# Modulation rows summed in PSUM under the down stages, and eight more up tiles as seven block products

## The chip, the cores and the metric

One core of one Trainium2 chip runs the whole program in one launch. The metric is the device time of an execution in microseconds; the kernel before has a median of 2543.47 us over three runs (2543.4 to 2543.87).

## What is computed

A sequence of 512 tokens of width 1024 passes two layers and a second block. Each layer has a gated FFN (width 2816), a mixer (attention in layer 0, a spatial gating unit in layer 1) and a second gated FFN; each of the three is preceded by an RMS norm that is scaled and shifted by rows of a modulation vector, and followed by a gate from the same vector. All arithmetic is float32.

```
c_act = silu(c)
for i in range(2):
    mod = c_act @ ada_w[i] + ada_b[i]            # 9 rows of 1024: shift, scale, gate, three times
    sh1, sc1, g1, sh2, sc2, g2, sh3, sc3, g3 = split(mod, 9)
    h = rms_norm(x, ln_ffn1[i]) * (1 + sc1) + sh1
    x = x + 0.5 * g1 * ((silu(h @ wg) * (h @ wu)) @ wd)
    ...                                          # mixer with sh2, sc2, g2; second FFN with sh3, sc3, g3
    x = rms_norm(x, ln_out[i])
```

The second block (a gated recurrence, an MLP with squared relu, a last norm) is not touched by the change, nor are the mixers.

## The kernel before

**Tiles.** A float32 product is made of three TensorE products of rounded parts: `hi*hi`, `hi*lo`, `lo*hi`. A weight tile is 1024 x 256, 1 MB. SyncE (SP) loads it to one of two slots of `w_raw`, ACT casts it to `w_hi_t` (`conv`, `cast_piece`, L1110, L1123), GpSimd (POOL) subtracts to get `w_lo_t` (L931, L937). The token operand is held as `h_hi` and `h_lo`, the FFN's hidden layer as `act_hi` and `act_lo`. A standard tile (`unit`, L2320 to L2325; at some places `unit_part`, L2337 to L2342) is two units of 24 products with 512 columns.

**Seven block products.** The other form of an up tile (`seven_tile`, L2377 to L2380) cuts weights and tokens into 2 x 2 blocks and makes seven products of blocks instead of eight, in the manner of Strassen: 84 TensorE products with 256 columns. In return other engines add blocks. On the weights: pieces 3, 4 and 6 of a tile (counted from 0) are sums made by DVE (`piece_sum`, L1818 to L1822) in PSUM banks 6 and 7, cast by ACT (`cast_piece`) and split by DVE (`piece_low`, L1828). On the tokens: four turned operands `t_hi_t` and `t_lo_t` are made once per FFN (`t_op`), in the down stage before the first such tile (`turns`) or, in a group of both forms, beside its standard tiles. On the results: ACT copies block results out of PSUM to `hidden` as they come (`snap`, L1131 to L1137), DVE adds them (`row_sum`). Product 3 of a tile waits for the copy of its product 0, product 6 for the fourth copy. `seven_act` writes out ACT's order: the copies of a tile alternate with the casts of the next tile's pieces; for the first tile of a stage, pieces 4 to 6 are cast at the end of the down stage, before the first copy.

**FFN stages.** An FFN goes through its 2816 hidden columns in three groups of 8, 8 and 6 up tiles (gate and up weights in turn), each followed by a down stage of four tiles that adds to `x`. Each unit of a down stage ends in one bank; DVE adds it to `x` (L2025), eight updates per stage, and TensorE may use the bank again two units later. In the loop over these updates `down` on DVE also has what is hung onto single updates: modulation steps, the turning, and, after updates 5 and 7 (counted from 0) where seven-product tiles follow, the first tile's pieces. `std` in the plan says how many tiles of a group are standard: all 22 in layer 0's first FFN, 8 (the first group) in layer 0's second and layer 1's first, 4 in layer 1's second.

**Modulation.** Sixteen rows of 1024 (`ada_block`) remain after the start. Each is summed by DVE in eight steps: SP loads 128 x 1024 of `ada_w` (512 KB) to one of four slots of `ada_raw`, DVE multiplies it with a column of `c_act` and adds it to an accumulator in `scr` (`ada_step`, L1678 and L1681). After the eighth step DVE transposes blocks (L1688) and reduces (L1689); TensorE adds over partitions (`ada_sums`, L2501), and DVE adds the bias and derives gains (`ada_fin`). The steps lie in the up stages of layer 0's first FFN (24, 24, 16), its first two down stages (12, 12), the first up stage of layer 0's second FFN (24) and of layer 1's first (16). The accumulators and slots lie in the part of `scr` that the turned operands use later, so these groups have standard tiles.

**Order.** Every engine runs one list in order, written out by the loops over `ops`; semaphores tie the lists. SP's list has the weight loads and the steps' loads in one queue. In layer 1's first FFN DVE also scales `x` by the last norm (`scale_x`, L1809), three blocks after each pair of up tiles.

## Time and profile before

| | |
|---|---|
| median of 3 runs | 2543.47 us |
| the profiled execution | 2543.58 us |
| its span, first to last instruction | 2541.7 us |
| TensorE busy | 2500.6 us, 98% |
| DVE, ACT, POOL busy | 58%, 44%, 44% |
| granted TensorE clock, mean | 0.994 |
| DMA | 312.52 MB, 123 GB/s over the span |
| modulation loads | 128 of 512 KB, 6.1 us to landing |

Times in the profile are microseconds from the span's start unless marked ns. PE is TensorE, POOL is GpSimd, SP is SyncE. In a timeline a line is: start, duration, engine, line, operation, output<-inputs, shapes, count, and in brackets the idle time of the engine before it and who ended it. Matmuls are pipelined, so start-to-start spacing is what one costs, not its duration.

### The profile page before, as it was taken

To read this page: it belongs to the slowest core of one execution; us is meant where nothing else is said; L and a number is where in the kernel's file an instruction comes from. 1 tells how busy PE (TensorE), PEld (TensorE's weight loads), DVE (VectorE), ACT (ScalarE), POOL (GpSimd) and SP (SyncE) were. 2 spreads that over 40 slices of the span, in tenths; PEclk is the share of its full clock that TensorE was granted. 3 is DMA by queue.
4 is the path that set the end of the run, shared out by engine and by line. 5 is a ranking of instruction groups with operands and counts; after the bars stand their busy time and mean duration, and the time that the engine had idled before them with its cause. 6 is when DMAs were issued, how large, how long until landed. Compare 5 with 4: busy or idle time off the path is not lost.

```text
span 2541.7 us, 36310 instructions
## 1 busy us (share of the span) xinstructions
PE 2500.6 (98%) x14578; PEld 2182.6 (86%) x14578; DVE 1466.4 (58%) x2045; ACT 1109.9 (44%) x1933; POOL 1112.6 (44%) x578
## 2 busy tenths in 40 slices
PE   6999999999999999999999999999999999999999
PEld 5888888776888989889998988999988888889998
DVE  6767674445577635767455258453566555564543
ACT  3222224565523635425445335454554444434544
POOL 2455444232446655456564435565640000455553
PEclk8999999999999999999999999999999999999999
DMA  8687754221372333543323322333232221223322
GB/s 297 223 274 244 244 195 129 67 67 50 116 243 90 115 100 96 180 139 100 114 86 100 118 83 67 117 100 133 92 101 86 67 67 50 92 92 114 103 84 83
DMA packets 249244, 312.52 MB, mean 123 GB/s; under 512 B 7356, under 2 KB 227149, under 8 KB 248950
## 3 DMA queue, kind: packets, MB, share of 16 engines
q1 hardware_dynamic: 246762, 308.88, 36.9%
q8 instruction: 116, 1.90, 0.3%
q10 hardware_dynamic: 2316, 1.33, 0.2%
q14 instruction: 50, 0.41, 0.1%
HBM read 308.07 MB, written 4.74 MB: 123 GB/s over the span
## 4 chain that ended last, share of the span: by engine, by line
PE 92%; DVE 4%; DMA 1%; issue 1%; ACT 1%; POOL 0%; SPq 0%; DVEq 0%; ACTq 0%
PE bank L2320 12%; PE bank L2325 12%; PE bank L2321 12%; PE bank L2377 8%; PE bank L2380 8%; PE bank L2378 8%; PE bank L2337 6%; PE bank L2338 5%; PE bank L2342 5%; PE bank L2303 2%; PE bank L2305 1%; PE bank L2304 1%; PE bank L2392 1%; PE bank L2393 1%; PE bank L2394 1%
## 5 line engine op out<-in xcount | busy, mean ns | idle before, releaser
L937 POOL TENSOR_TENSOR w_lo_t<-w_raw,w_hi_t 128x1024 fp32r<-128x1024 f32 (+1 forms) x284 | 713.9, 2531 | 1163.4 <-ACT w_hi_t L1110 1162.9
L1110 ACT CAST w_hi_t<-w_raw 128x1024 fp32r<-128x1024 f32 (+1 forms) x316 | 311.1, 1026 | 368.5 <-PE bank L2325 175.7
L931 POOL TENSOR_TENSOR w_lo_t<-w_raw,w_hi_t 128x512 fp32r<-128x512 f32 x232 | 323.3, 1409 | 240.3 <-ACT w_hi_t L1123 238.1
L2320 PE MATMUL bank<-act_hi,w_hi_t 128*128 128x512 f32 x720 | 280.9, 390 | 1.5 <-DVE x L2025 1.3
L2320 PE MATMUL bank<-h_hi,w_hi_t 128*128 128x512 f32 x720 | 281.3, 391 | 0.6 <-ACT hidden L1377 0.6
L2321 PE MATMUL bank<-act_lo,w_hi_t 128*128 128x512 f32 x720 | 280.2, 389 | 0.0
L2321 PE MATMUL bank<-h_lo,w_hi_t 128*128 128x512 f32 x720 | 280.2, 389 | 0.0
L1681 DVE SCALAR_TENSOR_TENSOR scr<-scr,cact 128x1024 f32<-128x1024 f32 x112 | 215.0, 1920 | 62.8 <-DMA scr<-in_ada_w 54.8
L2377 PE MATMUL bank<-t_hi_t,w_hi_t 128*128 128x256 f32 x928 | 232.8, 283 | 0.0
L2378 PE MATMUL bank<-t_lo_t,w_hi_t 128*128 128x256 f32 x928 | 232.7, 283 | 0.0
L2025 DVE SCALAR_TENSOR_TENSOR x<-bank,half,x 128x512 f32<-128x512 f32 x88 | 65.9, 749 | 222.8 <-PE bank L2325 152.5
L1123 ACT CAST w_hi_t<-bank 128x512 fp32r<-128x512 f32 x174 | 102.3, 588 | 189.8 <-PE bank L2325 63.4
L2325 PE MATMUL bank<-act_hi,w_lo_t 128*128 128x512 f32 x720 | 178.7, 389 | 0.1
L2377 PEld LDWEIGHTS bank<-t_hi_t,w_hi_t 128*128 128x128 f32 x928 | 178.2, 192 | 0.0
L2378 PEld LDWEIGHTS bank<-t_lo_t,w_hi_t 128*128 128x128 f32 x928 | 178.2, 192 | 0.0
L2325 PE MATMUL bank<-h_hi,w_lo_t 128*128 128x512 f32 x720 | 177.8, 389 | 0.0
L2377 PE MATMUL bank<-h_hi,w_hi_t 128*128 128x256 f32 x696 | 174.5, 283 | 0.0
L2378 PE MATMUL bank<-h_lo,w_hi_t 128*128 128x256 f32 x696 | 174.5, 283 | 0.0
L1123 ACT CAST w_hi_t<-w_raw 128x512 fp32r<-128x512 f32 x232 | 142.6, 623 | 71.7 <-PE bank L2325 53.2
L1828 DVE TENSOR_TENSOR w_lo_t<-bank,w_hi_t 128x512 fp32r<-128x512 f32 x174 | 119.9, 689 | 91.5 <-ACT w_hi_t L1123 88.2
L2320 PEld LDWEIGHTS bank<-act_hi,w_hi_t 128*128 128x128 f32 x720 | 135.1, 188 | 32.0 <-DVE x L2025 3.1
L2320 PEld LDWEIGHTS bank<-h_hi,w_hi_t 128*128 128x128 f32 x720 | 135.2, 188 | 29.2 <-ACT hidden L1377 1.0
(316 smaller groups left out, 5727.3 us busy)
## 6 DMA issues: line engine op xcount, KB each, us to landing
scr<-in_ada_w SPq DMA_DIRECT2D x128, 512.0 KB, 6.1
w_raw<-in_ffn_wg SPq DMA_DIRECT2D x44, 1024.0 KB, 5.4
w_raw<-in_ffn_wu SPq DMA_DIRECT2D x44, 1024.0 KB, 5.3
w_raw<-in_ffn_wd SPq DMA_DIRECT2D x32, 1024.0 KB, 5.3
w_raw<-in_mlp_w SPq DMA_DIRECT2D x32, 1024.0 KB, 5.3
w_raw<-in_hgrn_w_in SPq DMA_DIRECT2D x16, 1024.0 KB, 5.4
w_raw<-in_ffn_wd SPq DMA_DIRECT2D x16, 768.0 KB, 4.4
w_raw<-in_attn_w_qkv SPq DMA_DIRECT2D x12, 1024.0 KB, 5.1
```

Source lines behind the costliest of these rows:

```text
L931: nc.gpsimd.tensor_tensor(piece(w_lo_q, t, j), raw_quarter(t, n, k), piece(w_hi_q, t, j).bitcast(F32), ALU.subtract).then_inc(w_lo, 1)
L937: nc.gpsimd.tensor_tensor(w_rows(w_lo_t, t, k.start, k.stop), w_raw[:, t % 2, k], w_rows(w_hi_t, t, k.start, k.stop).bitcast(F32), ALU.sub ...
L1110: act.copy(w_rows(w_hi_t, t, k.start, k.stop), w_raw[:, slot, k]).then_inc(w_hi, 1)
L1123: act.copy(piece(w_hi_q, t, j), src).then_inc(w_hi, 1)
L1681: dve.scalar_tensor_tensor(acc, src, cact[:, kb:kb + 1], acc, ALU.mult, ALU.add).then_inc(ada_ch, 1)
L2320: pe.matmul(dst, w, blk(m_hi, kb), start=kb == 0, stop=False)
L2321: pe.matmul(dst, w, blk(m_lo, kb), start=False, stop=False)
L2325: last = pe.matmul(dst, w_at(w_lo_t, t, kb, b * P, (b + 1) * P), blk(m_hi, kb), start=False, stop=kb == kbs - 1)
L2337: pe.matmul(dst, w, blk(m_hi, kb), start=kb == 0, stop=False)
L2377: pe.matmul(dst, w_h[:, kb], m_hi[kb], start=j < 3 and kb == 0, stop=False, skip_group_check=True)
L2378: pe.matmul(dst, w_h[:, kb], m_lo[kb], start=False, stop=False, skip_group_check=True)
L2380: mm = pe.matmul(dst, w_l[:, kb], m_hi[kb], start=False, stop=kb == 3, skip_group_check=True)
```

## The change

Plan: the first FFN's up stages carry 32, 0, 0 steps and its first two down stages 16 each, all its tiles stay standard. In layer 0's second FFN and layer 1's first the first group is 4 standard and 4 seven-product tiles; its up stages carry no step, the first two down stages 16 each. `turns` no longer falls on a down stage of these FFNs; the turning lies beside the four standard tiles.

Step: two halves of 512, the sum in two PSUM banks (4 and 7 under up tiles, 2 and 3 under down tiles), the eighth step's result back into the slot in SBUF, where it is transposed (to `sq`). The four slots move to another part of `scr`. In a down stage two steps follow each x update. SP puts 5, 4 and 4 of their 16 loads behind the stage's second, third and fourth weight tile and 3 behind the first pair of the next up stage. Sums on TensorE and their reading on DVE come in eight places instead of five: at the end of the first up stage, and after the first tile of later down stages. TensorE waits for the reductions before it uses banks 2 and 3 again.

```diff
+class Fin:
+
+
+    def __init__(self, count, groups):
+        self.count, self.groups = count, groups
+        self.layer, m = ada_block(groups[0])
+        self.m0, self.m1 = DB * m, DB * (m + len(groups))
+        self.slot = groups[0] if groups[0] < 4 else groups[0] % 2
+        self.bank = 6 if groups[0] == 0 else 1
...
 def down_steps(op, nb):
-    return range(op.c0 + min(2 * nb, 4 + nb), op.c0 + min(2 * nb + 2, 5 + nb))
+    return range(op.c0 + 2 * nb, op.c0 + 2 * nb + 2)
...
-            ffn(layer, "ffn1", 0, (24, 24, 16), down_ada=(12, 12, 0))
+            ffn(layer, "ffn1", 0, (32, 0, 0), (8, 8, 6), down_ada=(16, 16, 0))
         else:
-            ffn(layer, "ffn1", 0, (16, 0, 0), (8, 0, 0))
+            ffn(layer, "ffn1", 0, (0, 0, 0), (4, 0, 0), down_ada=(16, 16, 0))
...
-            ffn(layer, "ffn2", 2, (24, 0, 0), (8, 0, 0))
+            ffn(layer, "ffn2", 2, (0, 0, 0), (4, 0, 0), down_ada=(16, 16, 0))
...
+            while summed < c // 8:
+                layer = ada_block(summed)[0]
+                groups = [g for g in range(summed, c // 8) if ada_block(g)[0] == layer]
+                summed, fin = groups[-1] + 1, fin + 1
+                op.fins.append(Fin(fin, groups))
...
-        ada_acc = scr[:, 0:4096].rearrange("p (g n) -> p g n", g=4)
-        ada_t = scr[:, 8192:9216]
-        ada_raw = scr[:, 4096:8192].rearrange("p (s n) -> p s n", s=4)
+        ada_t = sq[:].rearrange("p b n -> p (b n)")
+        ada_raw = scr[:, 8192:12288].rearrange("p (s n) -> p s n", s=4)
...
-        pre_rstd = scr[:, 11776:11776 + S]
+        pre_rstd = rstd[:]
...
                 if s >= 4:
-                    sp.wait_ge(ada_ch, s - 3)
+                    if s % 8 == 3:
+                        sp.wait_ge(ada_red, (s - 3) // 8)
+                    sp.wait_ge(ada_ch, 2 * (s - 3))
...
+            owed, staged = (), 0
...
+                    for step in owed:
+                        ada_step(step)
+                    owed = ()
...
-                                for nb in ((), (0, 1), (2, 3), (4, 5, 6, 7))[2 * i + s]:
-                                    for step in down_steps(op, nb):
-                                        ada_step(step)
+                                if i == 0 and s == 1:
+                                    sp.wait_ge(x_upd, op.x0)
+                                    if staged:
+                                        sp.wait_ge(t_ok, 4 * staged)
+                                k0, k1 = ((0, 0), (0, 5), (5, 9), (9, 13))[2 * i + s]
+                                for step in range(op.c0 + k0, op.c0 + k1):
+                                    ada_step(step)
+                                owed = range(op.c0 + 13, op.c0 + 16)
...
+            def ada_step(s, banks):
+
+                src, kb, g = ada_raw[:, s % 4, :], s % 8, s // 8
                 dve.wait_ge(ada_in[s % 4], 16 * (s // 4 + 1))
-                if kb == 0:
-                    if s >= 32:
-                        dve.wait_ge(ada_red, s // 8 - 3)
-                    dve.tensor_scalar(acc, src, cact[:, kb:kb + 1], None, ALU.mult).then_inc(ada_ch, 1)
-                else:
-                    dve.wait_ge(ada_ch, s)
-                    dve.scalar_tensor_tensor(acc, src, cact[:, kb:kb + 1], acc, ALU.mult, ALU.add).then_inc(ada_ch, 1)
+                for hf in range(2):
+                    part, acc = src[:, hf * S:(hf + 1) * S], ps[banks[hf]][:]
+                    if kb == 0:
+                        ins_ = dve.tensor_scalar(acc, part, cact[:, kb:kb + 1], None, ALU.mult)
+                    else:
+                        dve.wait_ge(ada_ch, 2 * (s - 1) + hf + 1)
+                        ins_ = dve.scalar_tensor_tensor(acc if kb < 7 else part, part, cact[:, kb:kb + 1], acc,
+                                                        ALU.mult, ALU.add)
+                    ins_.then_inc(ada_ch, 1)
                 if kb == 7:
-                    g = s // 8
-                    k = g - next(o.groups[0] for o in ops if o.groups and g in o.groups)
-                    dve.wait_ge(ada_ch, s + 1)
+                    k = g if g < 4 else g % 2
+                    dve.wait_ge(ada_ch, 2 * (s + 1))
                     if g:
                         dve.wait_ge(ada_red, g)
-                    link(dve.transpose(ada_t, acc))
+                    link(dve.transpose(ada_t, src))
                     dve.tensor_reduce(ada_r[:, 32 * k:32 * k + 32], ada_t.rearrange("p (c i) -> p c i", i=32),
                                       mybir.AxisListType.X, ALU.add).then_inc(ada_red, 1)
...
+            def summed(fin):
+
+                names = {1: ("g", 0), 2: ("h", 0), 4: ("g", 1), 7: ("g", 2), 8: ("h", 2)}
+                derive = [names[m] for _, m in map(ada_block, fin.groups) if m in names]
+                ada_fin(fin.layer, fin.m0, fin.m1, fin.count, derive, fin.bank)
...
+                            if pre_norm and op.t0 == pre_norm.t0:
+                                scale_x(pre_norm, range(3 * i, min(3 * i + 3, DB)))
                             continue
-                        for s in ada_steps(op, i) if op.ada else ():
-                            ada_step(s)
+                        steps = ada_steps(op, i) if op.ada else ()
+                        for s in steps[:6]:
+                            ada_step(s, (4, 7))
...
+                            if b == 0:
+                                for s in steps[6:]:
+                                    ada_step(s, (4, 7))
...
+                    if op.fins and op.fins[0].count == 2:
+                        summed(op.fins[0])
...
                         ins_.then_inc(x_upd, 1)
+                        for fin in op.fins if nb == 1 else ():
+                            if fin.count > 2:
+                                summed(fin)
                         for step in down_steps(op, nb) if op.ada else ():
-                            ada_step(step)
+                            ada_step(step, (2, 3))
                         if op.turns:
...
+            def ada_sums(fin):
+
+                n = DB * len(fin.groups)
+                pe.wait_ge(mod_ok, fin.count - 1)
+                pe.wait_ge(ada_red, fin.groups[-1] + 1)
+                own = ada_r[:, 32 * fin.slot:32 * fin.slot + 4 * n].rearrange("p (n q) -> p q n", q=4)
                 for q in range(4):
-                    part = ada_r[:, 0:4 * n].rearrange("p (n q) -> p q n", q=4)[:, q, :]
-                    mm = pe.matmul(ps[7][32 * q:32 * q + 32, op.m0:op.m0 + n], fold[:], part, start=True, stop=True)
+                    mm = pe.matmul(ps[fin.bank][32 * q:32 * q + 32, fin.m0:fin.m0 + n], fold[:], own[:, q, :],
+                                   start=True, stop=True)
                 mm.then_inc(ada_mm, 1)
...
+                                if i == 0 and s == 1 and rows:
+                                    pe.wait_ge(ada_red, rows)
...
+                                for fin in op.fins:
+                                    if fin.count > 2:
+                                        ada_sums(fin)
+                                rows = (op.c0 + op.ada) // 8 if op.ada else 0
```

On TensorE `ada_sums` is called with `after.fins[0]` at the end of the first up stage instead of with the op. ACT's and GpSimd's lists are unchanged in the code.

## Rows read from the trace of the kernel before

**Rows 1.** The page's first part: busy time of TensorE, share of the span, instructions.
```profile
PE 2500.6 (98%) x14578; PEld 2182.6 (86%) x14578; DVE 1466.4 (58%) x2045; ACT 1109.9 (44%) x1933; POOL 1112.6 (44%) x578
```

**Rows 2.** The page's chain that ended last, shares by engine.
```profile
PE 92%; DVE 4%; DMA 1%; issue 1%; ACT 1%; POOL 0%; SPq 0%; DVEq 0%; ACTq 0%
```

**Rows 3.** Timeline of PE (start, duration, line, operands), layer 0's second FFN, stage starts.
```profile
812.67 0.28 PE L2377 MATMUL bank<-h_hi,w_hi_t 128*128 128x256 f32 x1
...
893.30 0.40 PE L2337 MATMUL bank<-act_hi,w_hi_t 128*128 128x512 f32 x1
...
936.85 0.28 PE L2377 MATMUL bank<-h_hi,w_hi_t 128*128 128x256 f32 x1
...
941.16 0.28 PE L2377 MATMUL bank<-t_hi_t,w_hi_t 128*128 128x256 f32 x1
```

**Rows 4.** Timeline of PE, first group of that FFN: second tile, then down stage.
```profile
692.11 0.40 PE L2320 MATMUL bank<-h_hi,w_hi_t 128*128 128x512 f32 x1
...
768.59 0.50 PE L2337 MATMUL bank<-act_hi,w_hi_t 128*128 128x512 f32 x1
```

**Rows 5.** Timeline of PE, layer 1's second FFN, first group (4 standard, 4 seven-product tiles).
```profile
1550.51 0.40 PE L2320 MATMUL bank<-h_hi,w_hi_t 128*128 128x512 f32 x1
...
1624.75 0.40 PE L2337 MATMUL bank<-act_hi,w_hi_t 128*128 128x512 f32 x1
...
1668.30 0.28 PE L2377 MATMUL bank<-h_hi,w_hi_t 128*128 128x256 f32 x1
```

**Rows 6.** Groups of DVE by line: count, busy us, mean ns, idle before.
```profile
L1681 DVE SCALAR_TENSOR_TENSOR scr<-scr,cact 128x1024 f32<-128x1024 f32 x112 | 215.0, 1920 | 62.8 <-DMA scr<-in_ada_w 54.8 <-DVE scr L1681 0.5
...
L2025 DVE SCALAR_TENSOR_TENSOR x<-bank,half,x 128x512 f32<-128x512 f32 x88 | 65.9, 749 | 222.8 <-PE bank L2325 152.5 <-PE bank L2342 70.2
```

**Rows 7.** Timeline of DVE, the down stage of rows 3 and its end.
```profile
903.05 0.75 DVE L2025 SCALAR_TENSOR_TENSOR x<-bank,half,x 128x512 f32<-128x512 f32 x1 [6.23 <-PE bank L2342]
...
937.05 0.75 DVE L2025 SCALAR_TENSOR_TENSOR x<-bank,half,x 128x512 f32<-128x512 f32 x1 [4.69 <-PE bank L2325]
```

**Rows 8.** Timeline of DVE, end of layer 0's first FFN's second down stage.
```profile
312.39 1.27 DVE L1681 SCALAR_TENSOR_TENSOR scr<-scr,cact 128x1024 f32<-128x1024 f32 x1
313.70 1.25 DVE L1688 STREAM_TRANSPOSE scr<-scr 128x1024 f32<-128x1024 f32 x1
```

**Rows 9.** Timeline of ACT at the stage start 936.85.
```profile
939.09 0.59 ACT L1123 CAST w_hi_t<-bank 128x512 fp32r<-128x512 f32 x1 [0.94 <-DVE bank L1822]
...
940.10 0.37 ACT L1131 COPY hidden<-bank 128x256 f32<-128x256 f32 x1
```

**Rows 10.** Waits of PE: who for whom, us in total, times, longest.
```profile
PE bank L2320 <- DVE x L2025: 1.3, 2, 1.1
```

**Rows 11.** Timeline of SP, the down stage of rows 3.
```profile
910.32 0.37 SPq L769 DMA_DIRECT2D w_raw<-in_ffn_wg  x1
```

**Rows 12.** The page: a group of POOL, and a DMA issue (KB, us to landing).
```profile
L937 POOL TENSOR_TENSOR w_lo_t<-w_raw,w_hi_t 128x1024 fp32r<-128x1024 f32 (+1 forms) x284 | 713.9, 2531 | 1163.4 <-ACT w_hi_t L1110 1162.9
...
w_raw<-in_ffn_wd SPq DMA_DIRECT2D x32, 1024.0 KB, 5.3
```

**Rows 13.** Groups of DVE: `scale_x` in layer 1's first FFN (1060 to 1112), then all.
```profile
L1809 DVE SCALAR_TENSOR_TENSOR x<-x,vec,scr 128x512 f32<-128x512 f32 x8 | 16.3, 2083 | 0.0
...
L1809 DVE SCALAR_TENSOR_TENSOR x<-x,vec,scr 128x512 f32<-128x512 f32 x16 | 21.6, 1414 | 0.7 <-ACT scr L1250 0.7
```

**Rows 14.** Timeline of DVE, first seven-product tile of rows 5.
```profile
1589.11 1.71 DVE L1818 TENSOR_TENSOR bank<-w_raw 128x512 f32<-128x512 f32 x1 [0.50 <-POOL w_raw L927]
```

**Rows 15.** Timeline of ACT, the same tile.
```profile
1591.39 0.38 ACT L1137 COPY hidden<-bank 128x256 f32<-128x256 f32 x1
```

**Rows 16.** Timeline of DVE, end of the first FFN's first up stage.
```profile
130.13 1.22 DVE L1689 TENSOR_REDUCE ada_r<-scr 128x32 f32<-128x1024 f32 x1
```

**Rows 17.** Timeline of PE, the same place: sums, then the down stage.
```profile
135.19 0.28 PE L2501 MATMUL bank<-ada_r,fold 128*32 128x24 f32 x8
135.40 0.50 PE L2337 MATMUL bank<-act_hi,w_hi_t 128*128 128x512 f32 x1
```

More of the change, by code:

```diff
@@ L180, in make_plan @@
     t = x = n = h = v = a = c = 0
-    x, c, fin = 8, 0, 1
-    down, ups = None, []
+    x, c, fin, summed = 8, 0, 1, 0
+    down = None
     for op, then in zip(ops, ops[1:]):
@@ L191, in make_plan @@
             c += op.ada
-            ups.append(op)
-        elif op.kind == "adafin":
-            op.fin, fin = fin + 1, fin + 1
-            done = [g for g in range(c // 8) if not any(g in o.groups for o in ops if o.kind == "adafin" and o.groups)]
-            op.groups = done
-            op.layer = ada_block(done[0])[0]
-            ups[-1].fin, ups[-1].sums, ups[-1].m0 = op.fin, done, DB * ada_block(done[0])[1]
-            ms = [ada_block(g)[1] for g in done]
-            op.m0, op.m1 = DB * ms[0], DB * (ms[-1] + 1)
         elif op.kind == "upsq":
@@ L1707, in ada_fin @@
                     dve.scalar_tensor_tensor(gain[:, 0, 0, :], scale, 1.0, vec[:, V_LN:V_LN + DB], ALU.add, ALU.mult)
-                link(dve.tensor_tensor(mod[:, layer, m0:m1], ps[5 if count == 1 else 7][:, m0:m1],
+                link(dve.tensor_tensor(mod[:, layer, m0:m1], ps[bank][:, m0:m1],
                                        vec[:, V_ADA[layer] + m0:V_ADA[layer] + m1], ALU.add))
@@ L2558, in _ @@
             first_sums(ada_b_acc, 8, 8).then_inc(ada_mm, 1)
-            norm, npre, last_up = None, 0, None
-            for op in ops:
+            norm, npre, last_up, rows = None, 0, None, 0
+            for op, after in zip(ops, ops[1:] + [None]):
                 if op.kind == "norm":
@@ L2608, in _ @@
                             for b in range(2):
+                                if i == 0 and s == 1 and b == 0 and rows:
+                                    pe.wait_ge(ada_red, rows)
                                 if s == 0 and i:
@@ L2615, in _ @@
                                 unit(ps[2 * s + b][:], t, b, h_hi, h_lo, tile=None if b else t,
-                                     sums=op if op.ada and s == b == 1 and i == op.nb // 2 - 1 else None)
+                                     sums=after.fins[0] if op.ada and s == b == 1 and i == op.nb // 2 - 1 else None)
                 elif op.kind == "upsq":
```

24 lines of the change are left out of this document (4 added, 20 removed).

## The prediction

> **What bounds the kernel now.** I read the page first: TensorE (PE) is busy for 2500.6 us, 98% of the span [rows 1], and the chain of work that ended last lies 92% on it [rows 2]. So a change pays only by what it takes off TensorE's own stream, and costs whatever makes TensorE wait. Next the timeline of PE at the starts of stages, which prices a tile in either form: eight seven-product tiles run from 812.67 to 893.30, 10.08 us each, and the four standard tiles of the down stage after them to 936.85, 10.89 us each [rows 3]. A tile that becomes seven products saves 0.81 us. Last the timelines of VectorE (DVE) and ScalarE (ACT) where a stage of seven-product tiles begins, since there TensorE depends on both within a few microseconds.
>
> The profiled execution took 2543.58 us around a span of 2541.7, and the median shown is 2543.47; what I add to the span I add to 2543.5.
>
> **The eight tiles.** 8 x 0.81 = 6.5 us at most. What a group of 4 + 4 tiles really costs is shown by the second layer's second FFN, which has that form already: from its second tile, 1550.51, to its end, 1624.75, 74.24 us [rows 5]. The same stretch with eight standard tiles, in the first layer's second FFN, is 692.11 to 768.59, 76.48 us, its modulation sums included [rows 4]. So 2.24 us per FFN are gained, not 3.2: the turned operands (`t_op`) are then built beside the first standard tiles and hold something up. In return the first down stage loses that building: 43.55 us (1624.75 to 1668.30) [rows 5] against 44.08 (768.59 to 812.67) [rows 3, 4]. Both FFNs: 2 x (2.24 + 0.53) = 5.5 us gained. The bounds are 4.5 (the down stage gains nothing) and 7.5 (the tiles in full).
>
> **The modulation step on VectorE.** Before, a step is one 1024-wide multiply-add in SBUF, 1.92 us on the mean of 112 [rows 6]. After, it is two 512-wide ones with the sum in a PSUM bank, the operand kinds of the x update L2025, whose mean is 0.749 [rows 6] (issued back to back the next starts some 0.66 after: 2 x 0.66 = 1.3 us). Bounds: 1.27, the old step at its quickest [rows 8], and 1.92. I take 1.3, since L2025 is the nearer row.
>
> Under a down stage this is nearly free for seven of eight x updates. A unit takes 5.44 us (half of 10.89); update and two steps take 0.7 + 2.6; and TensorE needs an x update only when it reaches the unit after the next. After the fourth update the transpose (1.25) [rows 8] and reduction (1.22) [rows 16] of a finished row come on top: 5.8 us, late by 0.3, covered. The wait of 1.1 us that TensorE has for x [rows 10], in the second down of the first FFN, where a reduction now follows the second update, goes: -1.3 with the pipeline's refilling, bounds -1.3 and 0.
>
> **The last update before seven products.** Four down stages (the first two of the first layer's second FFN and of the second layer's first) now carry 16 steps, and an up stage of seven products follows at once. Call its start on TensorE U. Before, at U = 936.85 [rows 3], DVE's x update starts at 937.05 [rows 7]. Then `down` does `piece_low` of piece 4 and `piece_sum` of piece 6 (pieces count from 0); ACT, idle for 0.94 us until that sum (L1822), casts it at 939.09, then casts the next tile's piece 0, and only then takes the snapshot L1131 of TensorE's first product, 940.10 to 940.47 [rows 9]. TensorE's product 3 waits for that snapshot and starts at 941.16 [rows 3]. So the slack is 0.7 us, and ACT works in order: the snapshot can't pass the cast.
>
> After, `down` has the eighth update's two steps and the transpose and reduction of the second row between the x update and these pieces: 4 x 0.66 + 1.25 + 1.22 = 5.1 us. The sum of piece 6 moves from U + 2.1 to U + 7.2, the snapshot's end from U + 3.6 to U + 8.7, and TensorE, due at U + 4.3, waits 5.1 - 0.7 = 4.4 us. Nothing gives that back, since TensorE has no slack downstream; DVE and ACT catch up within the tile, so there is one wait per start. Four starts: +17.6 us. Bounds, by those of a step: 17.2 and 22.4.
>
> **What SyncE issues.** Every step is a 512 KB load on SP's queue, in line with the weights. In a down stage that starts on TensorE at D, the third tile's weights now queue behind the fifth step's load, which waits for the first step (its ring slot): the first x update at D + 9.75 (903.05 after 893.30) [rows 3, 7], + 0.7 + 1.3 = D + 11.8. With 1.3 us for that load and 5.3 for its own [rows 12] the tile lands at D + 18.4, and one cast (1.0) and two splits of 2.5 [rows 12] later, D + 24.5, it is whole; TensorE wants the first split half 16 products into the tile, D + 21.8 + 3.6. Covered by 1 us. The first weights of the next up stage, issued at D + 17.0 before (910.32) [rows 11], come after the thirteenth step's load, near D + 30, and land near D + 36: VectorE's first piece sum then waits some 2 us, which the gap up to the seventh update, at D + 38, mostly takes. I count 0, bounds 0 and 2.5 us at each of the four starts.
>
> **The scaling of x in the second layer's first FFN.** `scale_x` keeps its place after each pair of tiles, but the pairs now also carry the turning and the first pieces. Its eight instructions take 2.08 us each there, beside GpSimd's splits, while all 16 of the kernel have a mean of 1.41 [rows 13], so the other eight take 0.75. The first three delay the turned operands and the first piece sum: 3 x 2.08, less 2.9 us that the turning saves by then running clear of GpSimd, is 3.4 us, and as TensorE already loses time at that place in the like stage, ACT, which waits for the sum, passes about 1.9 us on. The second three come after the first seven-product tile's last piece and delay the next tile's first sum, 1589.11 in the like stage [rows 14], and so ACT's fourth snapshot, done at 1591.77 [rows 15], which TensorE wanted about 1 us later: 5.6 less that 1, and less the 0.9 net that TensorE itself is later, is 3.7 us. Together +5.6, bounds 0 (all six at 0.75) and 9.
>
> Here a page of the Trainium skill bears (SBUF — State Buffer, "Who interferes with whom"): a VectorE instruction with two SBUF inputs and a reading GpSimd instruction shut each other out for a whole instruction, and the order of issue decides which one waits. By that rule the six could as well go first, at 0.75 each, and the +5.6 would be about 0, the total 2558; the row's 2.08 says that most came second, and so I count them.
>
> **The first FFN.** Its tiles stay standard. Its first up has 32 steps instead of 24. The last reduction came at 130.13 to 131.35, 3.8 us before TensorE's sums at 135.19 [rows 16, 17]. Now eight steps go to a pair, the last two and a reduction between the two products of the pair; I put the fourth row's end at 23.4 us after the start of the last pair, where TensorE is done at 21.8: +1.7 with the refill, bounds 0 and 4. In the third down two sums follow one another, and the second waits for VectorE's reading of the first, which stands behind the second x update: +1.3, bounds 0 and 2. Sums on TensorE: eight instead of five, 0.2 us each [rows 17]; two of the five are already in the 76.48 and its like, so +1.0.
>
> **Sum.** -5.5 - 1.3 + 17.6 + 5.6 + 1.7 + 1.3 + 1.0 = +20.4 us: 2564.
>
> **Rivals.**
> A, covered starts: at the four starts VectorE's last block doesn't hold up the snapshot, and the x scaling finds gaps. For it: a down stage leaves DVE idle for 4.69 us before an update [rows 7]. Against: that idle time lies before the update, the block after it. Price: the 17.6 and 5.6 go, 2540.8, not slower than before; with the eight tiles whole and the first FFN without waits 2535. It decides at U + 4.3: whether TensorE's product 3 starts on time.
> B, the starts wait, the scaling doesn't: 2558. For it the 0.75 of the other eight scalings, against it the 2.08 of these.
> C, weights come late: 2.5 us more at each of four starts, 1 at the third tile of six downs: up to 16, so 2574 to 2580. For it SP's order; against it the 1 us of cover.
> D, the change doesn't do what it says: sums in PSUM cost 1.92 a step like those in SBUF, 4 x 1.2 more, 2569.
>
> **How the numbers follow.** Forecast 0.55, A 0.16, B 0.13, C 0.11, D 0.05. 0.2% (5 us) is about what a measurement of this kernel can tell from no change, so 2538.4 to 2548.6 is the same. A falls mostly there: faster 0.06, same 0.10, slower 0.84. The bounds of the terms give 2552 to 2576; reaching toward A and C the range is 2548 to 2577.
>
> **What would show it.** At each of the four starts after a modulated down: an idle time of PE of about 4.4 us before product 3 of the first tile, ended by ACT's snapshot L1131, and ACT before it idle until VectorE's sum; on DVE four half-steps of 0.75, a transpose and a reduction between x update and piece. In the second layer's first FFN, waits at its fifth and sixth tiles. In the first FFN's second down no wait for x. The forecast is wrong if those products start on time, or if the modulated downs themselves grow beyond 43.6 us.

## The result, and the profile after

2592.16 us (median; 2590.58 to 2593.22) against 2543.43 (2542.72 to 2543.87): slower, by a ratio of 1.0191, 95% interval 1.0174 to 1.0209. The direction is as forecast, the size is not: +48.7 us where +20.4 was forecast, 15 us over the range. The profiled execution has a span of 2588.7 us, 47.0 more than before, and its parts are taken from that. The table gives each stage by the starts of its first instructions on PE, the first FFN from its first product, 44.77 before (e6 and v3 are kernels of the experiments, put here for comparison):

| stage, us against the kernel before | forecast | after | e6 | v3 |
|---|---|---|---|---|
| first FFN, six stages | +2.3 | +13.6 | +10.5 | -0.4 |
| layer 0, second FFN: first up and down | -2.7 | -2.7 | -2.7 | -2.7 |
| its second and third up (two starts) | +8.8 | +17.4 | 0.0 | 0.0 |
| layer 1, first FFN: first up and down | +2.9 | +0.9 | +2.4 | -1.6 |
| its second and third up (two starts) | +8.8 | +17.6 | 0.0 | 0.0 |
| the four down stages behind these starts | +0.4 | +1.7 | +3.7 | +1.6 |
| all else | 0 | -1.4 | -1.2 | -1.8 |
| span | +20.4 | +47.0 | +12.6 | -5.0 |

Of "all else" after, -0.8 is the attention: there the kernel before has the granted clock at half for 3.4 us from 622.09, and the kernel after has not.

First the page after: busy time of the engines, and the chain that ended last (they answer to [rows 1, 2]).

```profile
PE 2506.3 (97%) x14890; PEld 2199.9 (85%) x14890; DVE 1450.9 (56%) x2243; ACT 1135.0 (44%) x2005; POOL 1094.7 (42%) x602
...
PE 80%; DVE 10%; DMA 3%; issue 3%; ACT 2%; POOL 1%; SPq 0%; DVEq 0%; ACTq 0%
```

VectorE has less to do than before (1450.9 us against 1466.4), yet its share of the chain rose from 4% to 10%, and DMA's from 1% to 3%. An engine that is busy for little more than half the time now ends waits. The table of PE's waits (who for whom: us in total, times, longest) says which:

```profile
PE bank L2401 <- ACT hidden L1142: 24.3, 4, 6.2
PE bank L2525 <- DVE ada_r L1700: 7.6, 1, 7.6
...
PE bank L2401 <- ACT hidden L1148: 2.5, 1, 2.5
PE bank L2344 <- ACT w_hi_t L1121: 2.5, 1, 2.5
...
PE bank L2401 <- POOL w_raw L938: 1.0, 1, 1.0
```

The first is the forecast wait, product 3 for the snapshot (L1142 after, L1131 before), four times, but of 6.1 us each and not 4.4. The second stands in the first FFN's first up stage, where 1.7 was forecast. The third is the scaling of x; the fourth and fifth are weights that came late. One of the four starts on VectorE's timeline, U = 955.59 (it answers to [rows 7]; L2046 is the x update, L1835 to L1839 are piece sums):

```profile
951.02 1.70 DVE L1835 TENSOR_TENSOR bank<-w_raw 128x512 f32<-128x512 f32 x1 [2.72 <-POOL w_raw L938]
953.43 0.69 DVE L1845 TENSOR_TENSOR w_lo_t<-bank,w_hi_t 128x512 fp32r<-128x512 f32 x1 [0.71 <-ACT w_hi_t L1134]
954.04 0.69 DVE L1837 TENSOR_TENSOR bank<-w_raw,bank 128x512 f32<-128x512 f32 x1
954.64 0.74 DVE L2046 SCALAR_TENSOR_TENSOR x<-bank,half,x 128x512 f32<-128x512 f32 x1
955.30 2.72 DVE L1691 SCALAR_TENSOR_TENSOR bank<-scr,cact,bank 128x512 f32<-128x512 f32 x4
957.93 0.74 DVE L2046 SCALAR_TENSOR_TENSOR x<-bank,half,x 128x512 f32<-128x512 f32 x1
958.59 1.40 DVE L1691 SCALAR_TENSOR_TENSOR bank<-scr,cact,bank 128x512 f32<-128x512 f32 x2
959.90 1.40 DVE L1691 SCALAR_TENSOR_TENSOR scr<-scr,cact,bank 128x512 f32<-128x512 f32 x2
961.34 1.25 DVE L1699 STREAM_TRANSPOSE sq<-scr 128x1024 f32<-128x1024 f32 x1
962.62 1.22 DVE L1700 TENSOR_REDUCE ada_r<-sq 128x32 f32<-128x1024 f32 x1
963.75 0.68 DVE L1845 TENSOR_TENSOR w_lo_t<-bank,w_hi_t 128x512 fp32r<-128x512 f32 x1
964.35 0.69 DVE L1839 TENSOR_TENSOR bank<-w_raw,bank 128x512 f32<-128x512 f32 x1
```

Read it from below. The sum for product 3 comes at 964.35, behind a block from 958.59 to 963.75: 5.2 us, the forecast 5.1. The eighth x update itself starts at 957.93, U + 2.3, where it was U + 0.2 before [rows 7]. It stands behind the seventh update's steps, that update behind the piece sums, and the first of these waited 2.72 us for GpSimd's raw sum, made at 949.63 from weights that had just landed. SyncE's queue shows why (DMA issues, first the start just read, then the end of the first up stage):

```profile
942.37 0.43 SPq L772 DMA_DIRECT2D w_raw<-in_ffn_wg  x1
...
126.44 0.38 SPq L772 DMA_DIRECT2D w_raw<-in_ffn_wd  x1
```

The next stage's first weights go out at U - 13.2; before it was U - 26.5 [rows 3, 11]. In the first up stage the down stage's first weights go out at 126.44, before at 122.14. Both stand behind loads of modulation rows that wait for a slot. What that does to the first up stage's end, on ACT, VectorE and PE:

```profile
134.88 1.99 ACT L1121 CAST w_hi_t<-w_raw 128x1024 fp32r<-128x1024 f32 x2 [13.36 <-DMA w_raw<-in_ffn_wd]
136.78 1.07 ACT L1388 ACTIVATE hidden<-bank 128x512 f32<-128x512 f32 x2
```
```profile
137.40 0.69 DVE L2005 TENSOR_TENSOR bank<-hidden,bank 128x512 f32<-128x512 f32 x1 [8.24 <-ACT hidden L1388]
...
142.03 1.22 DVE L1700 TENSOR_REDUCE ada_r<-sq 128x32 f32<-128x1024 f32 x1
```
```profile
143.39 0.34 PE L2525 MATMUL bank<-ada_r,fold 128*32 128x32 f32 x8 [7.64 <-DVE ada_r L1700]
```

ACT works in order: it sat 13.36 us in front of a cast whose weights were late, with the SiLU behind it; VectorE waited for the SiLU, and its last two steps and the reduction, which stand behind that product, ended 7.6 us after TensorE's last matmul. It answers to [rows 16, 17].

The last part isn't on any list of waits. The four starts again, in windows of 30 us from U (us, then busy us and instructions of PE, PEld, DVE, ACT and POOL; then the granted clock, DMA share, GB/s):

```profile
822.48:852.48 30.00, 24.16 (x181) 23.98 (x180) 21.12 (x30) 13.87 (x28) 16.66 (x13) 0.89 0.23 71
955.59:985.59 30.00, 23.65 (x177) 23.30 (x176) 21.45 (x31) 13.86 (x28) 16.24 (x13) 0.89 0.23 72
1198.17:1228.17 30.00, 22.86 (x175) 22.51 (x174) 21.67 (x30) 13.65 (x28) 16.50 (x13) 0.89 0.23 72
1332.02:1362.02 30.00, 23.83 (x182) 23.59 (x181) 21.73 (x32) 13.87 (x28) 16.82 (x13) 0.89 0.22 72
```

The granted clock is 0.89 in each: for 6.8 of the 30 us it stood at half, the lower of its two levels (1.2 GHz). It fell during the wait (the second at 964.60) and rose at 971.43, 4.8 us after PE's return:

```profile
959.61 0.28 PE L2401 MATMUL bank<-t_hi_t,w_hi_t 128*128 128x256 f32 x1
959.73 0.28 PE L2402 MATMUL bank<-t_lo_t,w_hi_t 128*128 128x256 f32 x1
959.85 0.64 PE L2404 MATMUL bank<-t_hi_t,w_lo_t 128*128 128x256 f32 x4
966.64 0.55 PE L2401 MATMUL bank<-t_hi_t,w_hi_t 128*128 128x256 f32 x1 [6.16 <-ACT hidden L1142]
967.00 0.42 PE L2402 MATMUL bank<-t_lo_t,w_hi_t 128*128 128x256 f32 x1
967.21 0.41 PE L2401 MATMUL bank<-t_hi_t,w_hi_t 128*128 128x256 f32 x1
```

A product's matmuls now follow at 0.21 us where it was 0.12. PE worked at half speed for 5.5, 4.8, 3.8 and 4.1 us behind the four waits and lost half of that, 9.1 us. Waits 24.3, clock 9.1, and 1.2 of two smaller waits: 34.6 of the 35.0; the rest is the pipeline's refilling.

### The profile page after: what moved, and what is told of

Its sections match the earlier page's. It is cut to its first block, busy times and chain, and to the rows that moved or that the text cites. A ratio compares the mean times of both kernels' runs of the same rounds, so it can differ in the third digit from the quotient of the medians.

```text
span 2588.7 us, 37336 instructions
## 1 busy us (share of the span) xinstructions
PE 2506.3 (97%) x14890; PEld 2199.9 (85%) x14890; DVE 1450.9 (56%) x2243; ACT 1135.0 (44%) x2005; POOL 1094.7 (42%) x602
## 4 chain that ended last, share of the span: by engine, by line
PE 80%; DVE 10%; DMA 3%; issue 3%; ACT 2%; POOL 1%; SPq 0%; DVEq 0%; ACTq 0%
PE bank L2401 8%; PE bank L2402 8%; PE bank L2404 8%; PE bank L2344 8%; PE bank L2349 8%; PE bank L2345 8%; PE bank L2361 5%; PE bank L2362 5%; PE bank L2366 5%; DMA w_raw<-in_ffn_wd 1%; PE bank L2327 1%; PE bank L2329 1%; DMA w_raw<-in_ffn_wg 1%; PE bank L2328 1%; DMA scr<-in_ada_w 1%
## 5 line engine op out<-in xcount | busy, mean ns | idle before, releaser
L948 POOL TENSOR_TENSOR w_lo_t<-w_raw,w_hi_t 128x1024 fp32r<-128x1024 f32 (+1 forms) x268 | 640.1, 2405 | 1178.0 <-ACT w_hi_t L1121 1177.6
L942 POOL TENSOR_TENSOR w_lo_t<-w_raw,w_hi_t 128x512 fp32r<-128x512 f32 x264 | 369.1, 1413 | 273.4 <-ACT w_hi_t L1134 270.8
L2401 PE MATMUL bank<-t_hi_t,w_hi_t 128*128 128x256 f32 x1056 | 268.5, 286 | 28.1 <-ACT hidden L1142 24.3
L2402 PE MATMUL bank<-t_lo_t,w_hi_t 128*128 128x256 f32 x1056 | 267.4, 285 | 0.0
L2344 PE MATMUL bank<-h_hi,w_hi_t 128*128 128x512 f32 x592 | 231.9, 392 | 2.5 <-ACT hidden L1388 2.5
L2345 PE MATMUL bank<-h_lo,w_hi_t 128*128 128x512 f32 x592 | 230.6, 389 | 0.0
L2402 PEld LDWEIGHTS bank<-t_lo_t,w_hi_t 128*128 128x128 f32 x1056 | 205.2, 194 | 0.0
L2404 PE MATMUL bank<-t_hi_t,w_lo_t 128*128 128x256 f32 x1056 | 171.4, 285 | 0.0
L2046 DVE SCALAR_TENSOR_TENSOR x<-bank,half,x 128x512 f32<-128x512 f32 x88 | 65.9, 749 | 175.3 <-PE bank L2349 101.9
L2349 PEld LDWEIGHTS bank<-act_hi,w_lo_t 128*128 128x128 f32 x720 | 135.0, 188 | 28.8 <-POOL w_lo_t L948 0.8
L2345 PEld LDWEIGHTS bank<-act_lo,w_hi_t 128*128 128x128 f32 x720 | 135.2, 188 | 27.7
```

The source lines that it names most:

```text
L942: nc.gpsimd.tensor_tensor(piece(w_lo_q, t, j), raw_quarter(t, n, k), piece(w_hi_q, t, j).bitcast(F32), ALU.subtract).then_inc(w_lo, 1)
L948: nc.gpsimd.tensor_tensor(w_rows(w_lo_t, t, k.start, k.stop), w_raw[:, t % 2, k], w_rows(w_hi_t, t, k.start, k.stop).bitcast(F32), ALU.sub ...
L2344: pe.matmul(dst, w, blk(m_hi, kb), start=kb == 0, stop=False)
L2345: pe.matmul(dst, w, blk(m_lo, kb), start=False, stop=False)
L2349: last = pe.matmul(dst, w_at(w_lo_t, t, kb, b * P, (b + 1) * P), blk(m_hi, kb), start=False, stop=kb == kbs - 1)
L2401: pe.matmul(dst, w_h[:, kb], m_hi[kb], start=j < 3 and kb == 0, stop=False, skip_group_check=True)
```

## The experiments

All changes are against the changed kernel unless said. The theories: VectorE's block makes the wait (as forecast); late weights on SyncE's queue make it, or add to it; PE's clock falls because of the wait.

**e1: pieces ahead of the steps.** At the eighth update `piece_low`, `piece_sum`, `piece_low` run before the two steps.

```diff
+                        if nb == 7 and after.std == 0:
+                            piece_low(after.t0, 4)
+                            ...
                         for step in down_steps(op, nb) if op.ada else ():
                             ada_step(step, (2, 3))
```

> The four starts of up stages behind a down stage with modulation rows: at the eighth x update VectorE runs the snapshot's part and the sum for product 3 first, and its two modulation steps, transpose and reduction (5.1 us) behind them. Theory 1 (the 5.1 us block ahead of the pieces makes the wait, and the wait makes the clock fall): the 6.2 us wait before product 3 shrinks to what the late eighth update alone makes, about 1.2 us; the next tile's first sum now comes 5.1 us later, so 1 to 3 us turn up before its product 3 or 6; the granted clock stays at full speed, which gives back 2.5 us at each start. Together about 19 us less than the changed kernel, 2573 us. Rival 1 (late weights on SyncE's queue make the wait, the block only lies beside it): most of the 6.2 us and the clock's fall stay, 2588 to 2592 us. Rival 2 (the clock falls for another reason than the wait, such as the rows' traffic): waits gone, fall stays, about 2583 us.

2577.08 us. PE's waits for the two snapshots:

```profile
PE bank L2401 <- ACT hidden L1148: 10.9, 5, 2.5
...
PE bank L2401 <- ACT hidden L1142: 3.9, 4, 1.0
```

The four waits before product 3 fell from 6.1 to 1.0 us, what is left of the late eighth update (still at U + 1.8 to U + 3.5) after the slack; the block moved on and holds up the fourth snapshot, 2.1 us at each start (the fifth L1148 is the scaling's 2.5). So the block's place decides. The clock was not left in peace, as I had expected: it was at half for 3.4 us after two of these four starts.

**e2: no loads for the later rows.**

```diff
             def ada_step(s):
+                if s >= 64:
+                    return
```

> Leaves out the 64 loads of modulation rows from the second FFN on (the steps still run, on what the four buffers hold, so these rows are wrong). Theory 1 (VectorE's block makes 4.4 us of each 6.2 us wait; the other 1.8 us are weights that come late behind the steps' loads on SyncE's queue): the raw sum of the weights and the eighth update come at the time of before, each of the four waits is about 4.4 us, and the time is 7 us less if the clock still falls at such a wait (2585 us), 17 us less if it holds (2575 us). Rival 1 (the late weights are the cause of the whole wait): waits under 1 us, 2558 us or less. Rival 2 (the loads have no part in it): 6.2 us stay, 2592 us.

2581.57 us, and the four waits are

```profile
PE bank L2404 <- ACT hidden L1144: 17.9, 4, 4.5
```

4.5 us each: the block's 5.2 less the 0.7 of slack, to within 0.1 of the forecast 4.4; the weights go out at U - 26.5 to U - 27.0, as before, and the eighth update starts at U + 0.2. The other 1.6 us of each wait belong to the loads' place in the queue (or to their traffic: this run takes both away; e6 below separates them). The clock still fell at all four, for 3.4 or 6.8 us, so the time lies between the two figures of theory 1.

**e3: short steps.** Steps of the last eight rows on 32 columns.

```diff
-                    part, acc = src[:, hf * S:(hf + 1) * S], ps[banks[hf]][:]
+                    n = S if s < 64 else 32
+                    part, acc = src[:, hf * S:hf * S + n], ps[banks[hf]][:, 0:n]
```

> Steps of the last eight rows work on 32 columns of each half and not on 512 (these rows are wrong); loads, waits, transposes and reductions stay. The block ahead of product 3's sum falls from 5.1 to about 2.9 us. Theory 1 (VectorE's block is the larger part of the wait): each of the four waits falls from 6.2 to about 4.0 us; 9 us less than the changed kernel if the clock falls all the same (2583 us), 19 us less if it doesn't (2573 us). Rival 1 (late weights alone): 6.2 us stay, 2592 us. Rival 2 (the loads wait for the steps through their four buffers, so that shorter steps also bring the weights in earlier): waits of about 2.2 us and no fall, 2566 us.

2569.31 us; waits of 2.5 us, below the 4.0 of theory 1 and near the 2.2 of rival 2:

```profile
PE bank L2402 <- ACT hidden L1142: 10.0, 4, 2.5
```

The block takes 3.2 us here (950.18 to 953.38 at the second start) and not 2.9; less 0.7 of slack that is the whole wait, so the late weights add nothing to it. VectorE at that start, U = 949.31:

```profile
943.25 1.71 DVE L1836 TENSOR_TENSOR bank<-w_raw 128x512 f32<-128x512 f32 x1 [3.19 <-POOL w_raw L938]
...
949.51 0.75 DVE L2047 SCALAR_TENSOR_TENSOR x<-bank,half,x 128x512 f32<-128x512 f32 x1 [1.21 <-PE bank L2350]
```

The weights are still late (they go out at U - 14.6, against U - 13.2 and U - 26.5), and the first piece sum still waits 3.19 us; but the two steps behind the seventh update are short now and don't carry this on, so the eighth is back at U + 0.2. So rival 2 was near on the size of the wait, but not in its way, since the weights come only 1.4 us earlier: late weights cost TensorE something where full steps stand behind the seventh update. On the clock it was wrong, which was still at half for 3.4 us at three of the four starts.

**e4: weights ahead.** In the first up stage the down stage's first weights are issued before the last pair's last five loads.

```diff
                         if i + 1 < op.nb // 2:
                             pair(i + 1)
+                        elif first:
+                            wd = tile_src("ffn1_wd", 0, 0, KB)
+                            weight(0, op.t0 + op.nb, wd[:, :, 0:TW], KB)
                         for s in steps[RING - 1:]:
```

> In the first up stage SyncE issues the down stage's first weights ahead of the last pair's last five loads of modulation rows; all else as in the changed kernel. Theory 1 (the 7.6 us wait for the reduction at the end of the stage comes from weights that were issued 4.3 us later than before, through ScalarE's in-order cast and the late SiLU): the wait falls to about 2 us, and the low clock around it (10 us at half) goes: 6 to 9 us less than the changed kernel, 2583 to 2586 us. Rival 1 (VectorE's last steps in the stage make the wait, whenever SiLU comes): the five loads now come later behind the weights, the wait stays at 7 us or grows, 2592 to 2594 us.

2582.77 us, 9.4 less. The wait for the reduction:

```profile
PE bank L2529 <- DVE ada_r L1704: 1.2, 1, 1.2
```

7.6 became 1.2, and no fall of the clock is left there. The up stage's excess went from 8.4 to 2.1 us and the down stage's from 5.4 to 2.0. So my +1.7 for the fourth row was right for what it looked at, and the weights' place in SyncE's queue, at which I had not looked in that stage, cost 6.3 there and 3.4 behind it.

**d1: the kernel before, with a dose of VectorE work** of 2 to 14 operations ahead of the eighth update's pieces; they write banks that are written again before they are read.

```diff
                         if nb == 7 and after.std == 0:
+                            for k in range(doses.pop(0) if doses else 0):
+                                link(dve.tensor_tensor(ps[2 + k % 2][:], sq[:, k % 2, :], ps[2 + k % 2][:], ALU.mult))
```

> The kernel before, with 2, 4, 6, 8, 10, 12 and 14 more VectorE operations of 128x512 (about 0.7 us each, they spoil the results) ahead of the eighth update's snapshot part and sum, at the starts of the seven stages whose first tile is of seven products. No modulation rows and no late weights there. Theory 1 (VectorE's delay alone makes the wait, less 0.7 us of slack, and a wait of some length alone makes the clock fall): waits before product 3 of about 0.7, 2.1, 3.5, 4.9, 6.3, 7.7 and 9.1 us, 34 us together; at the short ones no fall, at those from 4 to 6 us on a fall to half speed that costs 2 to 3 us more: about 2588 us. Rival 1 (the fall belongs to the rows' traffic): the same waits, no fall, about 2578 us. Rival 2 (VectorE has more than 0.7 us of room): waits shorter by as much each, under 2570 us.

2592.51 us in the one execution there is. Product 3 at the seven starts (in brackets PE's idle time):

```profile
817.41 0.36 PE L2380 MATMUL bank<-t_hi_t,w_hi_t 128*128 128x256 f32 x1 [0.75 <-ACT hidden L1131]
944.03 0.35 PE L2380 MATMUL bank<-t_hi_t,w_hi_t 128*128 128x256 f32 x1 [2.21 <-ACT hidden L1131]
1181.71 0.55 PE L2380 MATMUL bank<-t_hi_t,w_hi_t 128*128 128x256 f32 x1 [3.67 <-ACT hidden L1131]
1313.87 0.46 PE L2380 MATMUL bank<-t_hi_t,w_hi_t 128*128 128x256 f32 x1 [5.13 <-ACT hidden L1131]
1697.15 0.55 PE L2380 MATMUL bank<-t_hi_t,w_hi_t 128*128 128x256 f32 x1 [6.59 <-ACT hidden L1131]
1832.20 0.55 PE L2380 MATMUL bank<-t_hi_t,w_hi_t 128*128 128x256 f32 x1 [8.04 <-ACT hidden L1131]
2329.96 0.55 PE L2380 MATMUL bank<-t_hi_t,w_hi_t 128*128 128x256 f32 x1 [9.44 <-ACT hidden L1131]
```

Each further pair of operations adds 1.46 us (2 x 0.73), and the line meets zero at 0.7 us of delay: the slack of the prediction, measured. The stages grew by 1.0, 3.9, 6.5, 6.9, 9.4, 10.0 and 11.7 us: at the first by its wait and the pipeline's refilling (0.16), at the other six by 1.5 to 2.7 more than the wait and the refilling. In these six the granted clock was at half for 3.4 to 10.2 us, with no modulation row in sight. The wait brings the fall, the rows' traffic is not needed; but the fall's cost doesn't grow with the wait, and a short wait brings it or doesn't: after the 2.5 us for L1148 in layer 1's first FFN, the same wait in eight kernels, the clock stayed up in the changed kernel, e3, e4 and e5 and stood at half for 3.4 us in e1, e2, e6 and v1. What decides there stays open.

**e5 and e6: steps earlier, then their loads too.** e5 puts four steps ahead of the first update, where VectorE idles, two at each of six updates, and none at the seventh and eighth.

```diff
-    return range(op.c0 + 2 * nb, op.c0 + 2 * nb + 2)
+    ends = (0, 4, 6, 8, 10, 12, 14, 16, 16, 16)
+    return range(op.c0 + ends[nb + 1], op.c0 + ends[nb + 2])
```

> The changed kernel, with a row pair's sixteen steps earlier in their down stage: four ahead of the first update (VectorE idles there for 8 us), then two at each of the first six updates, none at the seventh and eighth. Theory 1 (where the block stands is the cause): the four waits before product 3 fall to what the late eighth update leaves (0 to 1.2 us), no fall of the clock there, 28 to 35 us less than the changed kernel: 2557 to 2564 us. The SyncE queue, whose loads wait for the steps, gets free earlier too, so the late weights go (theory 2, that they make 1.8 us of each wait). Rival 1 (VectorE has no room in these stages, wherever the steps stand): sixth to eighth update come late, waits of 4 us and more stay, 2575 us or more.

2567.3 us, short of the 2564 of theory 1. At each start 1.5 to 2.0 us were left, without a fall of the clock, and the down stages grew by up to 2.6. The rival seemed to have a point, until VectorE's timeline before a start:

```profile
805.46 1.41 DVE L1692 SCALAR_TENSOR_TENSOR bank<-scr,cact,bank 128x512 f32<-128x512 f32 x2 [0.53 <-DMA scr<-in_ada_w]
813.58 1.41 DVE L1692 SCALAR_TENSOR_TENSOR bank<-scr,cact,bank 128x512 f32<-128x512 f32 x2 [6.71 <-DMA scr<-in_ada_w]
814.90 0.74 DVE L2051 SCALAR_TENSOR_TENSOR x<-bank,half,x 128x512 f32<-128x512 f32 x1
```

VectorE isn't full; it waits 6.71 us for a load that SyncE issued behind the next stage's weights. e6 moves these loads:

```diff
-    k0, k1 = ((0, 0), (0, 5), (5, 9), (9, 13))[2 * i + s]
+    k0, k1 = ((0, 0), (0, 5), (5, 10), (10, 16))[2 * i + s]
...
-    owed = range(op.c0 + 13, op.c0 + 16)
+    owed = ()
```

> As the kernel with the steps earlier (2567.3 us), and the loads of a row pair earlier as well: sixteen of sixteen go out before the next up stage's first weights, where three stood behind them; VectorE waited up to 6.7 us for such loads. Theory (what is left at the four starts and in the modulated down stages there are steps that wait for their loads on SyncE's queue, not a full VectorE): late x updates go, 6 to 14 us less, 2553 to 2561 us, unless the next stage's weights now come late by the three loads (1.3 us each), which would give some back. Rival (VectorE is full there): 2565 to 2569 us.

2556.23 us. The same windows of 30 us from the four starts:

```profile
819.35:849.35 30.00, 30.00 (x252) 30.00 (x251) 20.75 (x30) 18.81 (x39) 20.74 (x16) 1.00 0.34 106
945.89:975.89 30.00, 30.00 (x252) 30.00 (x251) 20.77 (x30) 18.82 (x39) 20.76 (x16) 1.00 0.35 106
1181.03:1211.03 30.00, 30.00 (x252) 30.00 (x251) 20.81 (x30) 18.80 (x39) 20.73 (x16) 1.00 0.34 107
1305.64:1335.64 30.00, 30.00 (x252) 29.99 (x251) 20.74 (x30) 18.81 (x39) 20.73 (x16) 1.00 0.34 106
```

PE is busy for all of each, at full clock: 35 us became 0.0, with the same sixteen steps and the same traffic. So the traffic is not the cause. Nor are late weights by themselves: they still go out at U - 15.6 to U - 16.1, 11 us later than before, and with no step behind the last two updates the eighth starts at U + 0.2. This is the settling run for the starts; what e6 has left over the kernel before is the first FFN (+10.5), one wait of 1.6 us for x in a down stage, and in layer 1's first up stage the scaling, with a fall of the clock behind it.

**c1 and c2: repairs together.** c1 is e5 with e4's weights and the scaling moved; c2 is c1 with the loads of e6.

> The changed kernel's plan (32 steps in the first up stage, 16 under each of six down stages) with three repairs together: steps earlier in their down stage, the down stage's first weights ahead of the first up stage's last five loads, the scaling of x out of layer 1's first up stage (five blocks at the head of the first down stage, three behind its second update). Theory (three causes, each by itself): the single effects add up, 2567.3 less 9.4 for the weights less 3 for the scaling, 2553 to 2557 us; the 10 us over the kernel before are then VectorE's full down stages. Rival (they share a cause, so that the second repair gives less beside the first): 2559 us or more.

> As the kernel with the three repairs (2562.9 us), with the loads earlier in the same way. Theory (loads): its late x updates, 13 us of waits, mostly go: 2546 to 2554 us. Rival (a full VectorE): 2560 to 2565 us.

c1 took 2562.93 us: the effects did not add up, 8 us more than their sum, as the rival had it. c2, 2552.5 (2550.21 to 2555.97), gets 10.4 back and is still at 1.0035 (1.0024 to 1.0047) of the kernel before. The first FFN's first down stage shows why c1 missed: it grew by 7.4 us in c1 and 5.7 in c2, where e4 alone had 2.0. There e4's weights ahead of the five loads and e5's steps ahead of the updates meet: in c1 VectorE waits for steps' loads, which block the x updates behind them (6.28 us at the same step in c2):

```profile
154.44 1.42 DVE L1696 SCALAR_TENSOR_TENSOR bank<-scr,cact,bank 128x512 f32<-128x512 f32 x2 [6.08 <-DMA scr<-in_ada_w]
```

Where a step stands ahead of an update, the step's load has to be in time for the update.

**v1, v2, v3: the eight tiles with the rows spread.** v1 keeps seven-product tiles and PSUM banks; the first FFN has 24, 24, 16 steps in its up stages (the kernel before's plan), and the two later FFNs only 8 under each of two down stages, at their first four updates. v2 and v3 also move the scaling to the first down stage: all eight blocks ahead of its first update, or five there and three after the second.

```diff
-            ffn(layer, "ffn1", 0, (32, 0, 0), (8, 8, 6), down_ada=(16, 16, 0))
+            ffn(layer, "ffn1", 0, (24, 24, 16), (8, 8, 6), down_ada=(16, 16, 0))
...
-            ffn(layer, "ffn2", 2, (0, 0, 0), (4, 0, 0), down_ada=(16, 16, 0))
+            ffn(layer, "ffn2", 2, (0, 0, 0), (4, 0, 0), down_ada=(8, 8, 0))
...
+                    if pre_norm and op.t0 == pre_norm.t0 + 8:
+                        scale_x(pre_norm, range(DB))
```

> A version: the eight more tiles as seven products and the rows on PSUM banks as in the changed kernel, but the first FFN keeps 24, 24 and 16 steps in its up stages and 16 and 16 in its first two down stages, and in the two later FFNs only 8 steps stand under each of two down stages, at their first four updates. Theory: no block ahead of the pieces, so the four starts cost nothing; left are what the changed kernel showed as gains (2.2 and 0.5 us at each of the two stages) less the scaling in layer 1 (3.7 us) and the sums (0.4 us in each of four stages): 2540 to 2544 us. Rival 1 (the first FFN loses again, with 16 steps under its down stages): 2546 to 2555 us. Rival 2 (8 steps at the first four updates already make the later updates late): 2548 us or more.

> As the spread version, with the scaling of x in layer 1's first FFN moved from VectorE's work in the first up stage to the head of the first down stage, where VectorE idles for 8 us before its first update. Theory (the scaling's 3.7 us in that up stage and at its turn are VectorE's lateness): 3 to 5 us less than the spread version, 2536 to 2540 us. Rival 1 (the scaling now makes the first updates late and the wait only moves): same as the spread version.

> As the spread version with the scaling at the head of the first down stage, but five blocks there and three behind the second update. Theory (eight blocks at the head make the first update late by the 0.9 us seen at that place): that wait goes, 0.5 to 1.2 us less, 2538 to 2539 us. Rival (three scalings behind the second update make the next ones late): 2539 to 2541 us.

v1 2541.71 us (ratio 0.9995, 0.9986 to 1.0004), v2 2539.45 (0.9983, 0.9974 to 0.9993), v3 2539.04 (0.9983, 0.9974 to 0.9991). v2 and v3 beat both kernels, by 0.17%: the intervals lie below 1, though this is less than the 0.2% that the prediction called measurable. v2 was 2.3 us below v1, less than the 3 to 5 expected. In the profiles the up stage got 4.3 faster and the down stage 1.0 slower, but v1's profiled execution (2543.26, above its median) has a fall of the clock at the scaling's wait, from 1091.29; compared with the changed kernel, which has the same wait without a fall, the up stage's gain is 3.0. v3's gain over v2, 0.4, is below what the runs tell apart; its profile shows the wait for x down from 0.9 to 0.3.

```profile
PE 2495.4 (98%) x14890; PEld 2191.3 (86%) x14890; DVE 1456.8 (57%) x2243; ACT 1134.6 (45%) x2005; POOL 1094.8 (43%) x602
```

The same count of PE's instructions as the changed kernel, 10.9 us less busy: behind its first 50 us it has no stretch at half clock but the last 5.

## Why the prediction was wrong in size

- **The eight tiles, -5.5: right.** In layer 0's second FFN, where nothing else falls into these stages, -2.2 and -0.5, as worked out.
- **A step in PSUM, 1.3 us: right** (a step's two halves in 1.40, four halves in 2.72; one has 0.75), and with it the block of 5.1.
- **The block at four starts, 17.6: right as far as it went.** e2 has 4.5 each without late loads, d1 the slack of 0.7, e1 and e6 show that its place is the cause.
- **SyncE's queue, counted 0, bounds 0 to 2.5 a start: the first step that failed.** 1.7 at each start (6.7 of the 26.6 us by which the span missed). I saw that the first piece sum would wait some 2 us, and let the gap before the seventh update take it. It waited 2.72, and took 1.70 where it took 0.69 before (at 926.84). It began at U - 4.6 (before: U - 10.0), when the seventh update was already due (U - 5.2 before), so that update came at U - 1.0; and the two steps behind it, 2.7 us, which the prediction did not count there, put the eighth at U + 2.3. e2, e3 and e6 each take one part of this away and have the eighth at U + 0.2. Rival C had the weights late, at 0.11. And the 2576 that the prediction gives as the bounds of its terms leaves out the queue's own bound, four times 2.5; with it they reach 2586.
- **The first FFN, +1.7 and +1.3, bounds 4 and 2: the second.** The queue's order was worked out for the down stages and not for the first up stage, whose steps per pair grew too: 9.4 us by e4. The double sum cost 1.1 (forecast 1.3). The x wait went, as forecast.
- **No term for the clock: the third.** 9.1 us behind the four waits. The kernel before has no wait of PE over 1.6 us outside its start and one fall of the clock there, 3.4 us at half in the attention, so its trace hardly showed the price; a wait of 4.4 us was counted at 4.4.
- **The scaling, +5.6: too much.** 3.7 (+1.4 in that stage instead of -2.2). The first six now take 1.4 us each on the mean, not the 2.08 of [rows 13]: two took 0.74 and 0.83, four 1.78. They are in the trace one by one before as well, 0.74, 2.89, 2.88, so the 2.08 was a mean of two kinds. The Trainium skill (SBUF — State Buffer, "Who interferes with whom") has it that the order of issue decides which of two engines waits; two short and four long ones agree with some coming first and some second, and no run here tests the order.

Sum of the misses: 6.7 + 9.1 at the starts, 1.6 of small waits and refilling there, 11.3 in the first FFN, 1.3 in down stages, less 2.0 of scaling and 1.4 elsewhere: the 26.6 by which the span missed.

## What to carry to other kernels

Work on an engine with spare time is free only in the right place: sixteen steps that cost 35 us at the four starts when two stood behind each update cost nothing there with four ahead of the first update, none behind the last two, and their loads in time (e6; 2 us remained in one of the down stages ahead of them). When a ring of buffers shares a queue with weights, the queue is to be worked through for every stage that the ring's use changes, since a load that waits for its slot holds back all behind it. And a wait of TensorE is priced with the slow stretch after it: here 4 to 6 us of waiting cost about 2 more.

## What was not expected of the hardware

The granted clock fell after single waits of 2.2 us (1.6 us lost behind it) up to 9.4 us (2.1 lost, 10.2 us at half); between them the loss was 1.5 to 2.7 whatever the length. It also stayed at full after two waits of 2.5 us in the changed kernel, one of which brought a fall in four other kernels. Beside that, a piece sum from SBUF, L1835, took 1.70 us while GpSimd was splitting at the start shown above, and 0.69 and 1.02 at the same start of e5 and e6, a spread like the scaling's.
